# The state-space work beside the gate tiles, placed on other tiles and in another order

## The reference, cut to what matters

```python
u, q, k, v, q_idx, k_idx, w_idx, gate_a, gate_b = jnp.split(h @ w_in, splits, axis=-1)
y_ssm, s_re, s_im = s5_mixer(u, h0_re, h0_im, ssm_log_dt, ssm_a_re, ssm_a_im, ...)
y_a = (y_ssm @ glu_w) * jax.nn.sigmoid(y_ssm @ glu_v)
...
mixed = (jax.nn.sigmoid(gate_a) * y_a + jax.nn.sigmoid(gate_b) * y_b) @ w_out
```

## Time and profile before

| | |
|---|---|
| median of 3 runs | 3155.24 us (3145.66, 3155.24, 3155.26) |
| the profiled execution, its own time | 3145.66 us |
| its span, first to last instruction | 3143.9 us |
| TensorE matmul busy | 2910.3 us |
| VectorE busy | 1691.9 us, 54% |
| ScalarE busy | 1191.6 us, 38% |
| GpSimd busy | 379.2 us, 12% |
| mean granted TensorE clock | 0.955 |
| gate tiles, first layer | about 657 to 794 us of the span |
| gate tiles, second layer | about 2218 to 2358 us of the span |

### The profile page before, as it was taken

The page is one execution under the profiler, slowest core; times in us unless marked ns, Lnnn a source line. Parts: engine busy times, 40 slices in busy tenths (PEclk is TensorE's granted clock), DMA queues, the critical chain, the costliest instruction groups (busy, mean ns, idle before and its releaser), DMA issues. The chain is left out here.

```text
span 3143.9 us, 55982 instructions
## 1 busy us (share of the span) xinstructions
PE 2910.3 (93%) x21922; PEld 2715.4 (86%) x21922; DVE 1691.9 (54%) x3314; ACT 1191.6 (38%) x2019; POOL 379.2 (12%) x430
## 2 busy tenths in 40 slices
PE   6899999889999989999869999997999889999997
PEld 5899999789776689999848999997997766999997
DVE  5442346877768474223364424478777684732234
ACT  5532333445344243222254323344453432522221
POOL 2100000214015100000021000011240340100000
PEclk8999999899999999999979999989999999999998
DMA  7443442312123333232174434323221243232321
GB/s 241 133 150 107 135 145 78 125 48 62 48 78 109 103 105 87 77 98 83 51 234 128 147 105 145 124 77 125 55 61 50 76 128 103 83 97 84 104 73 62
DMA packets 452487, 324.09 MB, mean 103 GB/s; under 512 B 25113, under 2 KB 403345, under 8 KB 451546
## 3 DMA queue, kind: packets, MB, share of 16 engines
q1 hardware_dynamic: 446906, 296.60, 31.4%
q0 software_dynamic: 5408, 25.17, 2.4%
HBM read 310.48 MB, written 11.24 MB: 102 GB/s over the span
## 5 line engine op out<-in xcount | busy, mean ns | idle before, releaser
L1187 PE MATMUL PS<-h_hi,w_hi 128*128 128x260 f32 (+1 forms) x4000 | 840.6, 292 | 42.1 <-POOL h_lo L2678 28.3
L1187 PE MATMUL PS<-h_lo,w_hi 128*128 128x260 f32 (+1 forms) x4000 | 816.1, 286 | 0.0
L1781 DVE TENSOR_TENSOR lo_apart<-stage,w_hi 128x1024 fp32r<-128x1024 f32 (+2 forms) x448 | 498.5, 1147 | 432.8 <-ACT w_hi L779 425.8
L1187 PEld LDWEIGHTS PS<-h_hi,w_hi 128*128 128x128 f32 (+1 forms) x4000 | 629.6, 192 | 91.6 <-issue 72.9
L1187 PEld LDWEIGHTS PS<-h_lo,w_hi 128*128 128x128 f32 (+1 forms) x4000 | 627.4, 192 | 0.0
L779 ACT ACTIVATE w_hi<-stage 128x1024 fp32r<-128x1024 f32 (+3 forms) x586 | 541.8, 954 | 76.3 <-DMA stage<-in_mod_w 40.0
L1187 PE MATMUL PS<-h_hi,lo_apart 128*128 128x260 f32 x2816 | 570.3, 285 | 0.0
L1187 PEld LDWEIGHTS PS<-h_hi,lo_apart 128*128 128x128 f32 x2816 | 437.8, 190 | 0.0
L1925 DVE TENSOR_TENSOR hidf<-sil,PS 128x520 f32<-128x520 f32 x88 | 61.3, 696 | 420.9 <-PE PS L1187 420.9
L1187 PE MATMUL PS<-hid_lo,w_hi 128*128 128x260 f32 x1408 | 285.3, 284 | 0.0
L1187 PE MATMUL PS<-hid_hi,w_hi 128*128 128x260 f32 x1408 | 284.5, 283 | 0.0
(11 more groups left out here) (428 smaller groups left out, 4055.7 us busy)
## 6 DMA issues: line engine op xcount, KB each, us to landing
stage<-in_ffn_in SPq DMA_DIRECT2D x176, 512.0 KB, 3.8
stage<-in_mod_w SPq DMA_DIRECT2D x144, 512.0 KB, 4.7
stage<-in_w_in SPq DMA_DIRECT2D x72, 512.0 KB, 3.6
stage<-in_ffn_out SPq DMA_DIRECT2D x64, 384.0 KB, 3.3
stage<-in_ffn_out SPq DMA_DIRECT2D x64, 320.0 KB, 3.1
stage<-in_w_out SPq DMA_DIRECT2D x16, 512.0 KB, 3.5
x_hold<-xT SPq DMA_DIRECT2D x2, 2080.0 KB, 6.5
xT<-x_hold SPq DMA_DIRECT2D x2, 2080.0 KB, 8.2
```

Source lines behind the costliest of these rows:

```text
L1187: return nc.tensor.matmul(out, lhsT, rhs, start=start, stop=stop)
L1781: nc.vector.tensor_tensor(lows(ch)[:, ch.slot, 0:ch.elems], stage[:, ch.slot, 0:ch.elems], w_hi[:, ch.slot, 0:ch.elems].bitcast(FP32), ALU ...
```

## The change

It moves steps to other tiles and hooks and changes two waits; every instruction stays the same. On TensorE, `within_chunks(t)` goes from tile 4t + 3 (after block 3) to tile 4t + 2 (after block 5), `read_out(t - 1)` in tile 4t goes from block 1 to block 5, and in `drive(t)` the wait on `cnt_ready` goes ahead of all matmuls. On VectorE, `skipped(t)` goes from tile 4t + 3 to 4t + 2, and `powered_inputs(t + 1, ...)` from tile 4t to 4t + 2, r = 0 ahead of the selection step and r = 1 behind it. On ScalarE, `taps(t)` is cut in two, with `inputs_feature_major(t + 1, 1)` (or `relu_head(3)` in the last group) between the halves.

```diff
@@ ScalarE, tiles g % 4 == 3
                         if t < 3:
                             inputs_feature_major(t + 1, 0)
+                        taps(t, (0, 1))
+                        if t < 3:
                             inputs_feature_major(t + 1, 1)
                         else:
                             relu_head(3)
-                        taps(t)
+                        taps(t, (2, 3))
@@ TensorE, drive
                     if t:
                         pe.wait_ge(m_ready, 2 * t)
+                        pe.wait_ge(cnt_ready, 4 * t + 1)
                     for q in range(4):
                         for r in range(2):
                             mm(PS[:, 2, r, q * NCH:(q + 1) * NCH], BT4[:, r, q, :], U4[:, 4 * t + q, 0:NCH])
-                    if t:
-                        pe.wait_ge(cnt_ready, 4 * t + 1)
@@ TensorE, within_chunks
-                    pe.wait_ge(cnt_ready, 4 * t + 4)
+                    pe.wait_ge(cnt_ready, 4 * t + 3)
@@ TensorE, count
-                    if s < 16 and s % 4 == 3:
+                    if s < 16 and s % 4 == 2:
                         pe.wait_ge(t4_ready, s // 4 + 1)
@@ TensorE, the gate tiles
                     elif g % 4 == 0:
                         drive(t)
-                        hooks = {1: lambda: read_out(t - 1)}
-                    elif g % 4 == 3:
-                        hooks = {3: lambda: within_chunks(t)}
-                        if t < 3:
-                            hooks[0] = lambda: inputs_turned(t + 1, 0)
-                            hooks[4] = lambda: inputs_turned(t + 1, 1)
+                        hooks = {5: lambda: read_out(t - 1)}
+                    elif g % 4 == 2:
+                        hooks = {5: lambda: within_chunks(t)}
+                    elif g % 4 == 3 and t < 3:
+                        hooks = {0: lambda: inputs_turned(t + 1, 0), 4: lambda: inputs_turned(t + 1, 1)}
@@ VectorE, the gate tiles
                     if g % 4 == 0:
                         products(t)
+                    if g % 4 == 1:
+                        scans(t)
+                    if g % 4 == 2:
                         if t < 3:
                             powered_inputs(t + 1, 0)
-                            powered_inputs(t + 1, 1)
-                    if g % 4 == 1:
-                        scans(t)
-                    if g % 4 == 3:
                         skipped(t)
...
                     selection_step(g)
...
                     if g % 4 == 1:
                         turned_back(t)
+                    if g % 4 == 2 and t < 3:
+                        powered_inputs(t + 1, 1)
                     if g % 4 == 2 and t:
                         y_lower(t - 1)
```

More of the change, by code:

```diff
@@ L994, in inputs_feature_major, with taps @@
                     nc.scalar.activation(BT4[:, r].rearrange("p a b -> p (a b)"), PS[:, 3, 0, :], ACT.Copy).then_inc(bt_ready, 1)
-                def taps(t):
+                def taps(t, rows):
                     act.wait_ge(t4_ready, t + 1)
@@ L1001, in taps @@
                         act.wait_ge(zeros_ready, 1)
-                    for k in range(LC):
+                    for k in rows:
                         for q in range(4):
                             last = nc.scalar.activation(T4[32 * k:32 * k + 32, q, k:LC, :], kk[32 * q:32 * q + 32, 0:LC - k, :], ACT.Copy)
-                    last.then_inc(t4_copied, 1)
+                    if rows[-1] == LC - 1:
+                        last.then_inc(t4_copied, 1)
                 def y_upper(t, half):
```

## The result

The changed kernel takes 3212.44 us (median of 4 runs, 3207.81 to 3214.24), the kernel before 3155.25 us beside it on the same chip (3145.66 to 3160.78). The ratio is 1.0183, with a 95% interval of 1.017 to 1.0197: slower by 57 us. The profiled execution took 3208.58 us around a span of 3206.9, at a mean granted clock of 0.946 (0.955 before).

What follows compares the result with a forecast made beforehand. TensorE, busy for 93% of the span and nearly solid in the gate tiles, was taken as the bound. The terms 6.0 + 12.6 + 29 - 3.7 + 10 gave +54 us, 3203 us, with a range of 3172 to 3232.

Steps and rivals of the forecast that it cites:

- C: `inputs_turned(t+1, 0)` on TensorE waits for the second `powered_inputs`: 2.1 us, six times, 12.6 us.
- the clock: TensorE's granted clock drops at six places with stalls: 1.7 us each, 10 us; ends -5 and +20.
- CA: `within_chunks` may wait for GpSimd's CA, late through the later `read_out`: up to 1 us, not in the sum.
- The removed wait: `within_chunks` in tile 4t+2 asks for one selection step less: takes away at most 3.7 us of TensorE's waits.
- A: Wait on the counting at the head of `drive`, no longer hidden by 16 matmuls: 1.0 us, six times, 6.0 us.
- B: `count(4t+2)` waits for kk behind VectorE's queue: 2.9, 5.8 and 5.8 us a layer, 29 us in all.
- The disputed cost: First `powered_inputs` on VectorE beside GpSimd's `states`: 4.0 us if it waits out both operations, 1.6 alone.
- ScalarE: Taps cut in two around `inputs_feature_major(t+1, 1)`: free; half of the taps, 2.2 us, the price if not.
- B is small: VectorE's operations slip between GpSimd's, so the kk waits fall toward 3 us: +20 to +38, 3166 to 3184; chance 0.27.
- Low clock holds on: Two slow-clock stretches at each stall and `powered_outputs` 1 to 2 us later: +75 to +90, 3221 to 3236; chance 0.11.
- Only the wait goes: BX ready by hook 0 and the `drive` wait hidden: gains 3.7 us, perhaps 5.1 more, 3137 to 3142; chance 0.03.
- an even trade: Wait at `drive` offset by removed waits and saved slow stretches, rest mostly covered: within 10 us, 3145 to 3160; chance 0.04.

Runs made afterwards that it cites:

- experiment with the hook alone: Kernel before with `within_chunks` called after block 5 instead of block 3, still in tile 4t+3: 3155.00 us against 3153.22, ratio 1.0003.
- the eighth experiment: Kernel before with only `taps` cut in two around the second copy of BX: 3160.62 us against 3153.40, ratio 1.0022.
- second experiment: Kernel before with `powered_inputs(t+1)` moved to tile 4t+2, its halves around the selection step: 3194.60 us, ratio 1.012.
- third: Changed kernel with both halves of `powered_inputs(t+1)` back in tile 4t: 3175.07 us, ratio 1.0069 against the kernel before.
- fourth: Changed kernel with `skipped(t)` ahead of the first `powered_inputs` in tile 4t+2: 3210.68 us, ratio 1.0181 against the kernel before.
- the first experiment: Kernel before with only the `cnt_ready` wait moved ahead of all matmuls of `drive`: 3158.73 us against 3153.66, ratio 1.001.
- the sixth: Changed kernel with `read_out(t-1)` back at hook 1 of tile 4t: 3205.84 us, ratio 1.0164 against the kernel before.
- the ninth: Kernel of the fifth experiment with `taps` whole again, behind both copies of BX: 3159.90 us against 3153.40 for the kernel before, ratio 1.0022.
- the fifth experiment: Changed kernel with `powered_inputs`, `read_out` and the wait in `drive` put back: 3157.27 us against 3153.22 for the kernel before, ratio 1.0012.

## Why the prediction held, step by step

The forecast was +54 us, 3203; measured 3212.4 against 3155.2, +57, inside the forecast's own range (+38 to +75). The 3203 was reckoned from a value between two runs of before, 3145.66 and 3155.24; from the median the same sum gives 3209. The forecast held because every wait it named is in the trace, at its place. That the sum came within 3 us is in part luck: C was 4.2 us too large, and the clock and CA were 4.2 and 2.6 too small.

- **The removed wait, -3.7.** The waits for the counting are gone: 3.3 us of `within_chunks` and, which the forecast did not tell apart, 0.4 of `count(9)`. The experiment with the hook alone shows no gain that can be measured.
- **A, +6.0.** 0.93 us, six times: 5.6.
- **C, +12.6.** Smaller than forecast: 8.4. At t = 0 it is 1.85. At t = 1 and 2 it is 1.18, and the cause can be read in the rows: `count(6)` starts at 729.50 and the turning at 732.74, 3.24 us later; VectorE's call is ready almost as forecast (3.0 us after the count at t = 0, 3.2 here), but TensorE is there only 2.06 us after the count instead of 0.93, since the count and the six matmuls behind it run at 1.2 GHz. So less of the same delay is idle. The missing part was not gained; it is in the clock's row.
- **B, +29.** 29.3 us: 2.50 at t = 0 (2.9 forecast), 5.83 and 5.81 at t = 1 and 2 (5.8 forecast), and 0.49 at t = 3, where I had put nothing. The disputed cost, `powered_inputs` beside `states`, is 3.8 us (4.0 forecast). This is the place that the Trainium skill spoke to (SBUF — State Buffer, "Who interferes with whom"): 1.44 and 1.43 us for a product beside GpSimd against 0.35 without it agrees with a lock for whole instructions. The steps up to 5.8 held too, about a microsecond late on both sides, so that the difference is right (in part luck: TensorE is late by the 0.63 us for CA that the sum left out): counted from D = 697.72, the scans end at 22.4 (713.99 + 6.10; 21.3 forecast), kk at 31.6 (729.10 + 0.25; 30.8 forecast), and TensorE wants its count at 26.0 (729.50 less the 5.83; 25.0 forecast). The scans were priced at 5.7 us from rows in which GpSimd ended before they did; here GpSimd works to their end and they take 6.10.
- **CA, nothing to 1 us each.** Named but not in the sum; 0.63 us, four times, 2.6 in all.
- **The clock, +10.** +14.2, the term that was mis-sized. I took 1.7 us for each of six stretches and kept the three of before. The new ones lose 3.3 us each on average (20.0 / 6): each pair of stalls, one block apart, goes with a stretch of 8 to 11 rows instead of 4. By itself that is the upper end given for the term. Those of before vanished, 5.8 us, for a reason that no run shows, and only this brought the net near the forecast.
- **ScalarE, nothing.** Right in this kernel, where from `count(0)` on no wait of TensorE in the stage has ScalarE as its cause; the eighth experiment shows that the cut alone costs 7 us, since its cover is kk coming a tile earlier.

The sum of the measured parts is 5.6 + 8.4 + 29.3 + 2.6 - 3.7 + 14.2 = 56.4.

**The rivals.** "B is small" fell: VectorE's operations did not slip between GpSimd's. "Low clock holds on" was right about the length of the stretches, though not about GpSimd, which was 0.6 us late and not 1 to 2. Its +75 was not reached: it also had C at full size and the stretches of before still there. "Only the wait goes" and "an even trade" fell: the turning waits at all six places, and BX is never there by its hook.

**What the working should have had.** B and C were priced as two stalls with two causes. The second, third and fourth experiments show one debt: VectorE has some 3.8 + 1.6 us of `powered_inputs` to do between `scans` and the turning, and TensorE pays for it at the first place where it asks for anything behind it. In the kernel of the second experiment all of it is paid at BX (17.7 us a layer), in the fourth 12.9 at BX and 4.3 at kk, in the changed kernel 4.2 and 14.6. A forecast that adds stalls has to carry each one forward, as this one did for C (it counted C from the `count` that had already waited).

## What to carry to other kernels

A step that is early on an engine which is not the bottleneck is not waste: its distance to the reader is the cover, and moving it next to the reader sells that cover, here 41 us for a step of two 1.6 us calls made three times a layer. Before a step is moved, add up all that the engine's queue holds between the last input and the reader, at the durations that it has beside its neighbours for as long as they are at work, and compare it with the time in which the reader arrives. And a stall of a few microseconds on TensorE should be priced with what its clock does afterwards: here 14 us on top of 42.

## What was unexpected of the hardware

The stalls took the clock down for longer than the idle time. With 2.50 and 1.85 us of idle, one block apart, 1.2 GHz was granted from 687 to 693; with 5.83 and 1.18 us the clock fell during the first idle time and eleven rows were slow. The three short stretches of low clock after `drive` do not follow from the code around them alone: in the trace of before the second layer has them and the first, with the same code, has none. In the traces of the changed kernel and of the first experiment no `drive` of t = 1 to 3 has one, while the sixth, which differs from the changed kernel only in `read_out`, has five of six, and the kernels of the eighth and ninth have one in each layer. With one trace of each kernel, chance and the edit cannot be told apart; what starts one of these while TensorE is fully busy stays open.

The other point is how VectorE and GpSimd slow each other. The same eight scans took 2.63 us alone, 6.10 us in the changed kernel, 5.7 in the fifth experiment and 3.56 in the ninth, and the difference is for how long GpSimd works beside them. In the changed kernel it is at work on CA until 721.30, past the end of the scans, and they take 2.3 times as long as alone. In the fifth experiment GpSimd ends 5.1 us after the scans begin, in the ninth 1.4 us after. If only the time beside GpSimd is stretched by 2.3, an estimate from the two rows of 6.10 and 2.63, the scans should take 5.5 and 3.4 us, within 0.2 us of what they took. This is why a late start and the slow duration do not add up: scans that start late have less of GpSimd's work beside them.
